# A cumulated decay spread by a transfer instead of transposes, and sample states as the moving operand

## The reference

```python
gam = jnp.cumsum(g, axis=-1)                       # cumulated log decay
decay = jnp.exp(jnp.where(causal, gam[..., :, None] - gam[..., None, :], -jnp.inf))
a = jnp.where(strict, beta[..., :, None] * (k @ k.T) * decay, 0.0)
qk = (q @ k.T) * decay
qd = q * jnp.exp(gam)[..., None]
ko = k * jnp.exp(gam[..., -1:] - gam)[..., None]
u = vw - kd @ s                                    # s: state, kd from the triangular solve
o = qd @ s + qk @ u
s = exp(gam[..., -1]) * s + ko.T @ u
```

## Time and profile before

| | us |
|---|---|
| median of 3 runs (range) | 1057.51 (1057.25 to 1058.67) |
| the profiled execution, its own time | 1057.45 |
| its span, first to last instruction | 1055.7 |
| TensorE busy | 1038.3 (98%) |
| VectorE busy | 745.4 (71%) |
| GpSimd busy | 634.6 (60%) |
| ScalarE busy | 592.1 (56%) |

### The profile page before, as it was taken

One profiled execution on the slowest core, in us unless ns is written; L12 is line 12 of the kernel. 1 busy time (PEld: TensorE's weight loads), 2 busy tenths in 40 slices (PEclk: granted clock), 3 DMA queues, 4 the chain that ended last, 5 costly groups with the idle time before them and its releaser, 6 DMA issues.

```text
span 1055.7 us, 21847 instructions
## 1 busy us (share of the span) xinstructions
PE 1038.3 (98%) x7971; PEld 1012.8 (96%) x7971; DVE 745.4 (71%) x1254; ACT 592.1 (56%) x1105; POOL 634.6 (60%) x546
## 2 busy tenths in 40 slices
PE   8999999999999999999999999999999999999997
PEld 6999989999999999999999999999999999999997
DVE  7989898898888988889867757594544444444335
ACT  7855556575565755656646865765444443343632
POOL 1894686684876948768583443646555555555631
PEclk9999999999999999999999999999999999999999
DMA  6312212222122221322222162122222223222402
GB/s 239 105 68 81 95 42 92 84 80 95 40 91 84 79 95 40 93 81 90 88 77 61 43 250 80 41 70 97 98 96 81 81 83 114 82 79 79 116 7 89
DMA packets 32651, 92.08 MB, mean 87 GB/s; under 512 B 4688, under 2 KB 12240, under 8 KB 32592
## 3 DMA queue, kind: packets, MB, share of 16 engines
q1 hardware_dynamic: 32592, 91.29, 26.2%
HBM read 82.76 MB, written 8.52 MB: 86 GB/s over the span
## 4 chain that ended last, share of the span: by engine, by line
PE 80%; DVE 7%; POOL 4%; issue 3%; ACT 2%; DVEq 0%; ACTq 0%; POOLq 0%
PE ps L749 26%; PE ps L1162 15%; PE ps L1110 13%; PE ps L758 7%; PE ps L1194 5%; PE ps L714 3%; DVE ps L1908 3%; DVE t_r L1905 1%; PE ps L1006 1%; POOL in_lo L2601 1%; DVE work L2139 1%; PE ps L768 1%; POOL work L2601 1%; POOL w_lo L2601 1%; POOL o_a L2601 1%
## 5 line engine op out<-in xcount | busy, mean ns | idle before, releaser
L2601 POOL TENSOR_TENSOR w_lo<-raw,w_hi 128x1024 fp32r<-128x1024 f32 x100 | 241.2, 2414 | 157.0 <-ACT w_hi L1734 50.2
L749 PE MATMUL ps<-in_hi,w_hi 128*128 128x288 f32 x944 | 286.1, 303 | 1.1 <-ACT work L1408 0.6
L749 PE MATMUL ps<-in_lo,w_hi 128*128 128x288 f32 x944 | 282.3, 300 | 0.7 <-POOL in_lo L2601 0.7
L749 PE MATMUL ps<-in_hi,w_lo 128*128 128x288 f32 x944 | 282.7, 300 | 0.0
L1908 DVE SCALAR_TENSOR_TENSOR ps<-work,ct,ps 128x512 f32<-128x512 f32 x240 | 180.5, 752 | 7.1 <-DVE work L2068 1.6
L749 PEld LDWEIGHTS ps<-in_hi,w_hi 128*128 128x128 f32 x944 | 177.7, 188 | 2.7 <-issue 1.2
L749 PEld LDWEIGHTS ps<-in_lo,w_hi 128*128 128x128 f32 x944 | 177.3, 188 | 1.0 <-POOL in_lo L2601 0.9
L749 PEld LDWEIGHTS ps<-in_hi,w_lo 128*128 128x128 f32 x944 | 177.6, 188 | 0.5
L1905 DVE TENSOR_TENSOR o_a<-o_a,ps 128x576 f32<-128x576 f32 (+1 forms) x63 | 42.8, 681 | 107.3 <-PE ps L1162 73.1
L2601 POOL TENSOR_TENSOR w_lo<-t_pair,w_hi 128x1024 fp32r<-128x1024 f32 x18 | 43.6, 2422 | 42.5 <-ACT w_hi L1763 29.7
L1291 ACT CAST w_hi<-raw 128x1024 fp32r<-128x1024 f32 x63 | 65.6, 1043 | 0.2
(11 more groups left out here) (396 smaller groups left out, 2862.3 us busy)
## 6 DMA issues: line engine op xcount, KB each, us to landing
raw<-w_all_in SPq DMA_DIRECT2D x135, 512.0 KB, 3.7
work<-s_in_in SPq DMA_DIRECT2D x8, 512.0 KB, 3.4
s_sample_out<-work SPq DMA_DIRECT2D x8, 512.0 KB, 2.6
xt<-x_t_in SPq DMA_DIRECT2D x4, 576.0 KB, 6.4
xt<-x_t_in SPq DMA_DIRECT2D x2, 1152.0 KB, 7.1
y_out<-o_a SPq DMA_DIRECT2D x14, 144.0 KB, 1.9
halo<-halos_in SPq DMA_DIRECT2D x9, 156.0 KB, 3.5
conf_rows_out<-c_rows SPq DMA_DIRECT2D x8, 135.0 KB, 3.4
```

The costliest lines, as they stand in the source:

```text
L749: t = mm(dense_ps(n, j, h), a[:, w, k], b[:, k, h * HALF:(h + 1) * HALF], start=r == 0, stop=r == PASS_MM // 2 - 1)
L2601: return gp.tensor_tensor(out, a, b, op)
```

## The change

1. After the first stage, when the cumulated decay stands in `cols`, SP writes it to a device memory tensor `decay_rows` [8, 576] in five transfers of single float32 elements (4608 in all). From then on one transfer per pass reads the next head's row of 576 values and spreads it to 128 partitions, into `eg`, at the end of passes 1 to 7.
2. In passes 2 to 8 the five transposes of step 3 are gone. POOL subtracts `qk` from the spread row (512 and 64 columns) right behind the step that makes `qk`, in place; ACT takes all exponentials (576 columns of `eg`, then 512 and 64 into `dm`) in step 2 instead of steps 3 and 4. DVE's two subtractions of step 3 are gone. Step 5 of TensorE waits for `vt_ready` where step 3 did. Pass 1 keeps the transposes.
3. The eight products with the sample states have the states as the moving operand (128 columns). The weights are 32 columns of `um`, in which the q and the solved k of two samples stand side by side; the result of sample q goes to 32 partitions of PSUM of its own (partitions 0, 32, 64 or 96 on, two groups of 128 columns). POOL copies q into `um` in step 19 (64 columns), ACT writes the solved k there (with a wait for `tmi_ready`) and copies 256 columns instead of 64 out of PSUM.
4. The rows of such a result are picked out by products with 0/1 selection matrices: two of 128 columns and two of 64 in step 26, in place of the one with the identity. The matrices (128x384) are loaded once into a part of the constants that is free by then.

```diff
+                if first(n):
+                    sp.wait_ge(cum_ps, 1)
+                    sp.dma_start(sel_sb, sel).then_inc(consts_landed, 16)
...
+                    if n_is(n, 1):
+                        sp.wait_ge(log_dve, 6)
+                        gamma = cols[:, 40:80].rearrange("p (t h) -> p t h", t=TILES + 1)
+                        for t in range(TILES + 1):
+                            rows = min(P, TOK - P * t)
+                            sp.dma_start(decay_rows[:, P * t:P * t + rows].rearrange("h p -> p h"), gamma[0:rows, t],
+                                         allow_slow_non_contiguous=True).then_inc(log_landed, 16)
...
                     sp.wait_ge(ss_ready, n + 1)
+                    if not last(n):
+                        if n_is(n, 1):
+                            sp.wait_ge(log_landed, 112)
+                        row = decay_rows[n:n + 1] if isinstance(n, int) else decay_rows[bass.ds(n, 1)]
+                        sp.dma_start(v["eg"], row.to_broadcast([P, TOK])).then_inc(log_landed, 16)
...
-                    if s == 3:
+                    if n_is(n, 1) and s == 3:
...
                     if s == 5:
-                        pe.wait_ge(eg_ready, n)
+                        if n_is(n, 1):
+                            pe.wait_ge(eg_ready, 1)
+                        else:
+                            pe.wait_ge(vt_ready, n)
...
                         mm(g(1)[:, P:2 * P], wide("us"), v["vts"], start=True, stop=False)
-                        mm(g(1)[:, P:2 * P], wide("cs0"), con("ident"), start=False, stop=True).then_inc(us_ps, 1)
+                        both_halves = work[:, starts["cs0"]:starts["cs0"] + 2 * P]
+                        for h in range(2):
+                            r = mm(g(1)[:, P:2 * P], sel_sb[:, h * P:(h + 1) * P],
+                                   both_halves[:, h * P:(h + 1) * P], start=False, stop=h == 1)
+                        r.then_inc(us_ps, 1)
+                        for h in range(2):
+                            mm(g(2)[:, 0:SMP], both_halves[:, h * P:(h + 1) * P], sel_sb[:, 2 * P + h * SMP:2 * P + (h + 1) * SMP],
+                               start=h == 0, stop=False, skip_group_check=True)
...
-                            r = mm(two(g(2)[:, 0:2 * SMP])[:, :, q * LS:(q + 1) * LS], tile(v["ss"], q),
-                                   kq[:, :, SEQ + q * LS:SEQ + (q + 1) * LS], start=q == 0, stop=q == NS - 1,
-                                   skip_group_check=True)
+                            h, j = divmod(q, NS // 2)
+                            r = mm(g(2)[32 * j:32 * j + 32, P + h * P:2 * P + h * P], sample_pairs(q), tile(v["ss"], q),
+                                   start=True, stop=True, skip_group_check=True)
...
+                    if s == (3 if n_is(n, 1) else 2):
+                        act.wait_ge(dm_diff, n)
+                        if not n_is(n, 1):
+                            A(v["eg"], v["eg"], ACT.Exp).then_inc(eg_ready, 1)
+                        A(v["dm"][:, 0:SEQ], v["qk"][:, 0:SEQ], ACT.Exp)
+                        A(sm(v["dm"]), sm(v["qk"]), ACT.Exp).then_inc(dm_ready, 1)
...
-                        A(v["cs0"], g(2)[:, SMP:2 * SMP], ACT.Copy).then_inc(sz_ready, 1)
+                        A(work[:, starts["cs0"]:starts["cs0"] + 2 * P], g(2)[:, P:3 * P], ACT.Copy).then_inc(sz_ready, 1)
...
+                if not n_is(n, 1):
+                    pool.wait_ge(gm_ready, 2 * n - 1)
+                    pool.wait_ge(log_landed, 16 * n + 96)
+                    tt(v["qk"][:, 0:SEQ], v["eg"][:, 0:SEQ], v["qk"][:, 0:SEQ], ALU.subtract)
+                    tt(sm(v["qk"]), sm(v["eg"]), sm(v["qk"]), ALU.subtract).then_inc(dm_diff, 1)
...
-                        tt(pr(v["um"]), pr(t_r.bitcast(F32)), bc(con("ident")), ALU.subtract).then_inc(tmi_ready, 1)
+                        tt(pr(v["um"]), pr(t_r.bitcast(F32)), bc(con("ident")), ALU.subtract)
+                        gp.tensor_copy(sample_half(0), by_sample(v["qn"][:, SEQ:TOK])).then_inc(tmi_ready, 1)
```

More of the change, by code:

```diff
@@ L103, with build @@
 HALO = 3 * NS * (QK_TAPS - 1) + NS * (CF_TAPS - 1)
-def build(nc, x_t, w_all, w_log, log_par, consts, params, taps, halos, s_in,
+def build(nc, x_t, w_all, w_log, log_par, consts, params, taps, halos, s_in, sel,
           y_out, s_prompt, s_sample, qkv_rows, conf_rows):
@@ L189, in build @@
         ksq = v["extk"][:, 4:4 + TOK]
+        sel_sb = cst[:, OFF["tri"][0]:OFF["tri"][0] + 2 * P + 2 * SMP]
         q_sq = sb("q_sq", TOK)
@@ L296, in windows, with sample_pairs, sample_half, by_sample @@
             return bass.AP(v_.tensor, v_.offset, [v_.ap[0], [width, n], [1, LS], [1, taps]])
+        def sample_pairs(q):
+            first_ = SEQ + 2 * LS * min(q, NS - 2)
+            return v["um"][:, first_:first_ + 4 * LS]
+        def sample_half(a):
+            return v["um"][:, SEQ:SEQ + 2 * SMP].rearrange("p (q a t) -> p q a t", q=NS, a=2)[:, :, a]
+        def by_sample(ap):
+            return ap.rearrange("p (q t) -> p q t", q=NS)
         def products(i):
@@ L357, in build @@
         uc_ready = sem("uc_ready")
+        decay_rows = nc.dram_tensor("decay_rows", [H, TOK], F32, kind="Internal").ap()
         x_ps, x_ready, dt_ps, du_ps = sem("x_ps"), sem("x_ready"), sem("dt_ps"), sem("du_ps")
@@ L879, in phase @@
                         v_transpose_s()
-                    if s == 3:
[L882 to L886, removed]
+                    if n_is(n, 1) and s == 3:
+                        pe.wait_ge(hc_ready, 1)
+                        pe.wait_ge(pads_ready, 2)
                         for c in range(TILES):
@@ L1451, in phase @@
                         half_read(n, pos, j, 1)
-                    if s == 4:
+                    if s == 4 and n_is(n, 1):
                         A(v["eg"][:, 0:SEQ], g(1), ACT.Exp)
@@ L2092, in head @@
                     tt(smw(v["ko"]), g(2)[0:SMP, 0:P], hcol_s(KOF, P), ALU.mult).then_inc(gk_ready, 1)
-                if s == 3:
-                    dve.wait_ge(gam_ps, n)
-                    dve.wait_ge(gm_ready, 2 * n - 1)
-                    tt(v["dm"][:, 0:SEQ], g(1), v["qk"][:, 0:SEQ], ALU.subtract)
-                    tt(sm(v["dm"]), g(3)[0:SMP, 0:SMP], sm(v["qk"]), ALU.subtract).then_inc(dm_diff, 1)
+                if n_is(n, 1) and s == 3:
+                    dve.wait_ge(gam_ps, 1)
+                    dve.wait_ge(gm_ready, 1)
+                    tt(v["qk"][:, 0:SEQ], g(1), v["qk"][:, 0:SEQ], ALU.subtract)
+                    tt(sm(v["qk"]), g(3)[0:SMP, 0:SMP], sm(v["qk"]), ALU.subtract).then_inc(dm_diff, 1)
                 if s == 5:
@@ L2938, in shape_constants, with selections @@
     return out
+def selections():
+    row = np.arange(P)[:, None]
+    out = np.zeros((P, 2 * P + 2 * SMP), np.float32)
+    for h in range(2):
+        sample = 4 * h + row // 32
+        token, step = sample * LS + row % LS, row % 32 - np.where(sample == NS - 1, 2 * LS, 0)
+        out[:, h * P:(h + 1) * P] = (step >= LS) & (step < 2 * LS) & (token == np.arange(P)[None, :])
+        out[:, 2 * P + h * SMP:2 * P + (h + 1) * SMP] = (step >= 0) & (step < LS) & (token == np.arange(SMP)[None, :])
+    return out
 def channels(a):
@@ L3016 @@
         "s_in": f(state_delta)[0].transpose(1, 2, 0, 3).reshape(H, P, NS * P),
+        "sel": selections(),
     }
```

10 lines of the change are left out of this document (4 added, 6 removed).

## The result

| | before | after |
|---|---|---|
| median, us (range) | 1057.62 (1057.25 to 1058.67) | 1073.88 (1072.58 to 1076.25) |
| span of the profiled execution | 1055.7 | 1073.2 |
| pass 2 (first dense product to first dense product) | 118.6 to 188.6: 70.0 | 118.3 to 206.0: 87.7 |
| pass 5 | 319.8 to 385.2: 65.4 | 337.4 to 402.8: 65.4 |

The ratio is 1.0156 (95% interval 1.0143 to 1.0169): slower by 16.3 us, where 1051.0 was forecast. The table already has the two questions: all of the loss lies in pass 2, and the 0.8 us a pass that was to be gained is not there.

The account below looks back on a forecast made before the run. TensorE's own instruction time was taken to bound the passes (busy 98% at full clock). From 1057.45 us, -3.8 - 7.4 + 5.3 - 0.6 = -6.5 gave 1051.0; 8-in-10 range 1047.5 to 1058.5.

Parts of the forecast that it names:

- The transfers: Five first transfers of 4608 values and the row per pass: cost nothing; values landed at 122.1, upper bound 28 us.
- rival 3: The first store of the decay is late, delaying pass 2: 1054.3 us, or 1079 at the bound; chance 0.09.
- VectorE, ScalarE, GpSimd at the head of a pass: Moved subtractions, earlier exponentials and added copies are covered and cost nothing; a 0.57 us wait in pass 2 goes, saving 0.6.
- Transposes: Step 3, passes 2 to 8: removing five transposes saves 0.54 us a pass, 3.8 us in all.
- State products: Step 23, eight passes: sixteen instructions take 0.85 us instead of 1.78, saving 0.93 a pass, 7.4 us in all.
- the 0.7 to 1.0 that was to be the sign: Step 23 in the profile after: 16 instructions take 0.7 to 1.0 us from first start to next dense start.
- the reading of four slots: Step 23: first instructions run together, then second ones; four slots, 0.43 us, plus 0.3 for changes, 0.73.
- the one between two readings: Step 23: 0.85 us for 16 instructions, taken between nine slots, 0.96, and four slots plus changes, 0.73.
- Rivals 1 and 2: Step 23: column groups don't overlap, 1058.4 to 1060, chance 0.13; every instruction pays a tile change, bound 1071.3, chance 0.06.
- Selection products: Step 26, eight passes: six more instructions cost 0.67 us a pass, 5.3 us in all.
- Recurrence: VectorE's states for steps 23 to 26 come in time with the same cover of 0.65 us; cost nothing.
- rival 4: The recurrence adds a wait of 0.3 us a pass at the third or fourth state: 1053.4 us; chance 0.12.

Follow-up runs that it names:

- e12_late_reduce: The changed kernel with its store of single values where it was and the copy of the taps as a tensor_reduce; 1067.06 us, ratio 1.0089.
- e3_copy_form: The changed kernel with only VectorE's copy of the taps rewritten as a tensor_tensor maximum; 1071.69 us, ratio 1.0133.
- e11: As e12_late_reduce, but the five transfers of single values issued in pass 1 behind the load of the sample states; 1052.84 us, ratio 0.9952.
- e1_store_early: The changed kernel with only the five transfers moved from behind the halo load to behind the load of the selection constants; 1074.24 us, ratio 1.0152.

## Why the prediction was wrong

- **The transfers: the step that failed.** "I take zero, the nearest row" (25 ns a packet of 512 bytes). Measured: 96 ns a packet by the sum above, 66 by the like sum in e11. The values were to have landed by 122.1; SyncE's wait for their landing ended, and the row was issued, at 141.25 (137.84 in e12_late_reduce, 136.19 in e3_copy_form). The mechanism was there as rival 3, with bounds of 0 and 28 us and 0.09; it came at 14.4 us of waiting. Both ends were on record; what I had no reason for was to let the lower one decide. A 4-byte piece isn't like a 512-byte piece, and the bound of 1079 lay outside the range that I gave. A second error in the same step: I asked only when the row is wanted, not what becomes of the other transfers queued behind the values. In the change the next two issues took 5.55 and 13.18 us; in e1_store_early it was the halo load, and TensorE stood 13.34 us.
- **The clock.** I had no term for it: after the 14.4 us of standing the granted clock was 0.50 up to 154.0, which cost some 2.4 us more.
- **VectorE, ScalarE, GpSimd at the head of a pass ("All cost nothing"): wrong, 0.84 us in pass 5 and 4.7 us in passes 3 to 7 together.** I counted the two subtractions in GpSimd's time and found cover, and the exponentials did come early (ScalarE's at 345.62, 8.2 us after the pass began, where 330.91 was 11.1 after). What I didn't ask is which operation of VectorE now meets which operation of GpSimd. The trace of before had the sign: a copy of 12 columns that took 0.60. In pass 8 the same section failed a second time: the early exponentials bring a table load on ScalarE and a wait of 0.67 us in TensorE, where I had forecast no wait in steps 2 to 5.
- **Transposes: right,** 0.54 us a pass in the middle passes; in pass 8 the new wait takes it back.
- **State products: right,** 1.01 us gained against 0.93. From the first of the 16 instructions to the next dense start it is 0.57 us, below the 0.7 to 1.0 that was to be the sign; it is nearer to the reading of four slots (0.43) than to the one between two readings that I took. Rivals 1 and 2 fall.
- **Selection products: right,** 0.67. **Recurrence: right,** no wait at L1019 or L1030 in the middle passes, so rival 4 falls.
- **The sum:** with both faults mended the kernel takes 1051.86, and its middle pass 64.4 us where 64.6 was forecast. That the whole lies so near 1051.0 is in part luck. By the profiled executions passes 3 to 7 gain 4.7 us (4.0 forecast) and pass 2 gains 2.0 (1.4 forecast), but pass 8 loses 0.2, where it was to gain 0.8, and pass 2 starts 1.0 later, where it was to start 0.3 earlier.
- **The chances** don't follow from their parts: by the shares given to the rivals, "slower" is 0.065 + 0.06 + 0.045 = 0.17 and "same" 0.065, not 0.13 and 0.10.

## What to carry to other kernels

Price a transfer by its pieces, and let the worst bound decide when nothing in the trace has pieces that small; then look both at who waits for its landing and at what is queued behind it. Before moving an operation to GpSimd, lay VectorE's and GpSimd's timelines over each other and look for copies and two-input operations in SBUF that end exactly when GpSimd's operation does. Before moving an activation on ScalarE, look whether the functions on either side of it are the same in every pass, the last one too. Make the contiguous form first (here five small products and one store of 8 rows) and judge the rest of the change with it.

## What the hardware showed that I had not expected

- 4608 values of 4 bytes, issued from 111.14 us on, kept the 16 DMA engines nearly full up to 129 us and had all landed only at 141.2. An instruction fetch of 16 KB beside them took some 14 us instead of 1.0. TensorE's 1.49 us of "issue" up to 128.83 fell in that time; that it was such a fetch isn't shown.
- Four float32 products with 32 weight columns in different column groups run side by side: 16 instructions in 0.64 us, against 1.94 in one group.
- A VectorE copy of 12 columns takes 0.17 us with GpSimd idle and up to 2.75 beside it, ending 0.02 to 0.04 us after an operation of GpSimd's; it can let a second one pass first, as at 349.60.
- ScalarE loads a table for 1.28 us when its function changes between exponential and evacuation in pass 8; moving one activation ahead of another added such a load and 0.67 us of TensorE's time.
